# Four split slots instead of two for the weight parts of a two-block sequence model

## What is computed

```python
# first block, x [1, 512, 1024], mem [1, 256, 1024]
x = x + token_mixer(rmsnorm(x), w_in, ...)      # HGRN scan + mLSTM, two directions, @ w_out
x = x + cross_attention(rmsnorm(x), rmsnorm(mem), w_xq, w_xkv, w_xo)
x = x + square(relu(rmsnorm(x) @ w_up)) @ w_down
x = rmsnorm(x)
# second block
a = rmsnorm(x); proj = a @ w_in_2
y_att = windowed_gqa(rope(q), rope(k), v, sink) @ w_branch_attn
y_gla = gla_branch(...) @ w_branch_gla
h = x + (sigmoid(g_att) * y_att + sigmoid(g_gla) * y_gla) @ w_out_2
h = h + expert_choice_ffn(rmsnorm(h), ...)      # 16 experts, 64 tokens each
h = h + sigmoid(rmsnorm(h) @ w_ple_gate) * (p @ w_ple)
out = rmsnorm(h)
```

## Time and profile before

| what | value |
|---|---|
| median of 3 runs | 1978.03 us (1977.91 to 1978.99) |
| the profiled execution's own time | 1978.96 us |
| its span, first to last instruction | 1977.2 us |
| PE, POOL, DVE, ACT busy | 96%, 50%, 39%, 28% of the span |
| mean granted TensorE clock | 0.995 |

### The profile page before, as it was taken

One profiled execution on the slowest core, in us unless ns is written; L12 is line 12 of the kernel. 1 busy time (PEld: TensorE's weight loads), 2 busy tenths in 40 slices (PEclk: granted clock), 3 DMA queues, 4 the chain that ended last, 5 costly groups with the idle time before them and its releaser, 6 DMA issues.

```text
span 1977.2 us, 23272 instructions
## 1 busy us (share of the span) xinstructions
PE 1902.2 (96%) x9434; PEld 1394.3 (71%) x9434; DVE 778.3 (39%) x1187; ACT 554.4 (28%) x1122; POOL 994.2 (50%) x566
## 2 busy tenths in 40 slices
PE   7999998999999999999989999999999999999988
PEld 6888887688788888887867678887854444433436
DVE  2456668641423302433544365554241221221124
ACT  4535547331422101211133433342230000000025
POOL 5697867667278877887645496546600000000022
PEclk9999999999999999999999999999999999999999
DMA  5321124222133223222322222112699999999982
GB/s 183 96 75 43 44 75 139 85 73 98 33 96 96 96 96 96 96 96 86 119 64 64 65 77 84 54 64 75 270 362 421 421 421 422 420 421 421 421 348 74
DMA packets 92697, 335.81 MB, mean 170 GB/s; under 512 B 7696, under 2 KB 9488, under 8 KB 67760
## 3 DMA queue, kind: packets, MB, share of 16 engines
q1 hardware_dynamic: 88864, 321.29, 43.6%
q10 hardware_dynamic: 3584, 12.52, 1.7%
q0 software_dynamic: 144, 0.52, 0.1%
HBM read 328.01 MB, written 6.29 MB: 169 GB/s over the span
## 4 chain that ended last, share of the span: by engine, by line
PE 82%; DMA 7%; POOL 4%; DVE 3%; ACT 2%; issue 1%; SPq 1%; PEldq 0%; ACTq 0%; DVEq 0%; PEld 0%; POOLq 0%
PE bank L609 51%; PE bank L1867 12%; DMA arena<-in_w_exp_up 3%; PE bank L1898 3%; PE bank L786 2%; DMA shared<-in_w_exp_up 1%; DMA arena<-in_w_exp_gate 1%; DMA arena<-in_w_exp_down 1%; PE bank L630 1%; PE bank L1885 1%; POOL shared_r L667 1%; POOL shared_r L649 1%; PE bank L1071 1%; POOL shared_r L648 1%; PE bank L1453 1%
## 5 line engine op out<-in xcount | busy, mean ns | idle before, releaser
L609 PE MATMUL bank<-shared_r 128*128 128x512 f32 (+1 forms) x3888 | 899.0, 388 | 15.9 <-POOL shared_r L667 6.6
L609 PEld LDWEIGHTS bank<-shared_r 128*128 128x128 f32 x3888 | 704.8, 189 | 171.4 <-issue 16.7
L648 POOL TENSOR_TENSOR shared_r<-shared,small 128x1024 fp32r<-128x1024 f32 (+1 forms) x170 | 331.2, 1948 | 848.1 <-DMA shared<-in_w_ple_gate 493.7
L649 POOL TENSOR_TENSOR shared_r<-shared,shared_r 128x1024 fp32r<-128x1024 f32 (+1 forms) x170 | 419.3, 2466 | 13.4
L1867 PE MATMUL bank<-shared,arena 128*64 128x512 f32 x768 | 170.8, 595 | 9.5 <-DMA shared<-in_w_exp_gate 3.0
L1867 PE MATMUL bank<-arena 128*64 128x512 f32 x768 | 170.5, 595 | 9.8 <-DMA arena<-in_w_exp_up 4.0
L609 PE MATMUL bank<-shared_r,arena_r 128*128 128x512 f32 x768 | 176.1, 391 | 0.0
L609 PEld LDWEIGHTS bank<-shared_r,arena_r 128*128 128x128 f32 x768 | 144.2, 188 | 31.5
L667 POOL TENSOR_TENSOR shared_r<-shared,shared_r 128x1024 fp32r<-128x1024 f32 x42 | 106.9, 2547 | 76.8 <-ACT shared_r L658 76.7
L1867 PEld LDWEIGHTS bank<-shared,arena 128*64 128x64 f32 x768 | 57.4, 137 | 117.0 <-issue 106.6
L1867 PEld LDWEIGHTS bank<-arena 128*64 128x64 f32 x768 | 56.0, 137 | 117.3 <-issue 103.2
(11 more groups left out here) (429 smaller groups left out, 2086.1 us busy)
## 6 DMA issues: line engine op xcount, KB each, us to landing
shared<-in_w_in SPq DMA_DIRECT2D x80, 512.0 KB, 3.6
arena<-in_w_exp_gate SPq DMA_DIRECT2D x32, 1024.0 KB, 25.4
shared<-in_w_exp_gate SPq DMA_DIRECT2D x32, 1024.0 KB, 25.7
shared<-in_w_exp_up SPq DMA_DIRECT2D x32, 1024.0 KB, 23.4
arena<-in_w_exp_up SPq DMA_DIRECT2D x32, 1024.0 KB, 24.0
arena<-in_w_exp_down SPq DMA_DIRECT2D x32, 1024.0 KB, 25.5
shared<-in_w_exp_down SPq DMA_DIRECT2D x32, 1024.0 KB, 26.1
shared<-in_w_up SPq DMA_DIRECT2D x32, 512.0 KB, 3.6
```

Source lines behind the costliest of these rows:

```text
L609: ins = pe.matmul(dst, W_, x_, start=first, stop=final)
L648: link(pool.tensor_tensor(hi, raw(p), small[:, 18:19].to_broadcast([P, hi.shape[1]]), ALU.add))
L649: pool.tensor_tensor(lo, raw(p), hi.bitcast(F32), ALU.subtract).then_inc(S_("w_split"), 1)
```

## The change

Every weight part but those of the last stage gets one of four split slots instead of one of two. The two new ones lie in a new tile `spare` of 16 KB per partition. Its room comes from the descriptors' reserve, which is set to 1024 bytes per partition in place of the default, and from `arena`, shortened by 192 floats. `slot_free` waits for the part four before. The parts of `ple_gate` keep their slots and waits. The number of raw slots stays four, and no stream is reordered.

```diff
-ARENA = 26960
+ARENA = 26768
...
     X = sb("X", [P, ST, D])
+
+    spare_at = -(-nc.sbuf_base // 32) * 32
+    spare = sb("spare", [P, 2 * XPANEL])
+    spare_r = nc.alloc_sbuf_tensor_at("spare_r", [P, 2 * XPANEL], F32R, offset=spare_at)
...
             return arena_r[:, at:at + n], arena_r[:, at + n:at + 2 * n]
+        if p < late and parts[p]["split"] % 4 > 1:
+            at = 2048 * (parts[p]["split"] % 2)
+            return spare_r[:, at:at + n], spare_r[:, at + n:at + 2 * n]
         return shared_r[:, at:at + n], shared_r[:, at + n:at + 2 * n]
...
-        before = p - 6 if p >= late else split_parts[max(parts[p]["split"] - 3, 0)]
-        if parts[p]["split"] > 2 and (p < late or before >= late):
+        before = p - 6 if p >= late else split_parts[max(parts[p]["split"] - 5, 0)]
+        if parts[p]["split"] > 4 and (p < late or before >= late):
             part_done(eng, before)
...
-    nc = _bacc.Bacc("TRN2", target_bir_lowering=False, num_devices=1)
+    nc = _bacc.Bacc("TRN2", target_bir_lowering=False, num_devices=1, dynamic_dma_scratch_size=1024)
```

## The result

| kernel | median (range, runs) | ratio to before, 95% interval |
|---|---|---|
| before | 1978.65 us (1977.91 to 1980.93, 9) | |
| after | 1984.69 us (1983.22 to 1988.5, 9) | 1.0033 [1.0022, 1.0043] |

The profiled execution of the changed kernel took 1984.63 us (span 1982.9), 5.7 us more than that of the kernel before. Lines of the changed kernel are 7 higher than before: L616 is L609, L655 and L656 are L648 and L649, L674 is L667.

What follows compares the result with a forecast made beforehand. It took PE to bound the kernel, busy 1902.2 of 1977.2 us, with its waits for POOL's splits within reach. Gains 2.57 + 0 + 2.42 + 0.7 = 5.7 us took 1978.03 to 1972.3 us; range 1967.5 to 1978.0.

Steps and rivals of the forecast that it cites:

- the one behind `proj_a`: At DVE's rotation: it starts 1.0 us earlier, PE asks for it only afterwards, so the 2.42 us gain passes on.
- the four places: `proj_h`, `xk`, `proj_a` with `z`, and `gatt` with the start of `yatt`, where PE waits for POOL's splits.
- My own sign of being wrong: Matmuls from `spare_r` at 0.229 us or more, new PE waits in `hgrn` or attention, or a shifted DVE chain before `yatt`.
- `proj_h`, 2.57: In `proj_h`: both PE waits for POOL go, gaining 2.57 us, and `hgrn` behind it moves along; bounds 0 and 2.57.
- `xk`, 0: In `xk`: earlier splits meet the same DVE chain, gain 0; bounds a 2.5 us loss and a 3.6 us gain.
- the bound of one collision (2.5): In `xk`: the worst case, one more collision between POOL and DVE, costs 2.5 us.
- `proj_a` and `z`, 2.42: In `proj_a` and `z`: earlier splitting removes PE's waits of 0.85 and 1.25 us, gaining 2.42 us; bounds 1.01 and 2.42.
- `gatt` and `yatt`, 0.7: Before `yatt`: one 3.5 us wait replaces six small ones, gaining 2.35 us less 1.65 for half clock; other end 2.35.
- The reserve and the place of the halves, 0: Smaller descriptor reserve costs 0; reading half the parts from `spare` costs 0, bounds 0 and 5 to 17 us.
- The expert stage: Behind `ygla`: loads start when PE's `ygla` is evacuated, so its DMA and PE shift together.
- Splits move onto DVE's chain: Where DVE sets PE's pace, POOL's pair costs up to 4.3 us; slower from two places, 1980.9 us; chance 0.06.

Runs made afterwards that it cites:

- experiment 8: Changed kernel with the look-back of four parts only in `proj_h`, two elsewhere; 1975.99 us, 0.9988 of the kernel before.
- experiment 2: Changed kernel, but POOL splits two parts of `proj_g`, then waits until DVE has posted the rotation; 1977.22 us, 0.9991 of the kernel before.
- experiment 4: Changed kernel with the look-back of four parts only in `proj_a` and `proj_g`, two elsewhere; 1989.82 us, 1.0057 of the kernel before.
- experiment 6: Changed kernel with the look-back of four parts in `proj_h`, `down0` to `proj_a`, `gatt` and `yatt`, two elsewhere; 1971.34 us, 0.9956 of the kernel before.
- experiment 7: Changed kernel with the look-back of four parts only from `down0` to `proj_a`, two elsewhere; 1975.67 us, 0.9985 of the kernel before.
- experiment 9: Changed kernel with the look-back of four parts only from `down0` to `proj_g`, two elsewhere; 1985.42 us, 1.0036 of the kernel before.
- experiment 1: Changed kernel with its memory layout kept, but waiting for the part two before everywhere; 1978.54 us, 1.000 of the kernel before.
- experiment 3: Changed kernel with the look-back of four parts only in `proj_h`, `proj_a`, `gatt` and `yatt`, two elsewhere; 1976.17 us, 0.9984 of the kernel before.
- experiment 5: Changed kernel, look-back of four in `proj_h` and `down0` to `proj_r`, two elsewhere, POOL held in `proj_g` until the rotation is posted; 1972.45 us, 0.9962 of before.
- experiment 10: Changed kernel with the look-back of four parts only in `gatt` and `yatt`, two elsewhere; 1977.44 us, 0.9993 of the kernel before.

## Why the prediction was wrong, point by point

The step that failed is the one behind `proj_a`: "The rotation on DVE that follows ends at 990.4 ... and it starts from `proj_a`, so 1.0 us earlier ... the gain passes on". It started 0.6 us earlier (977.72 against 978.30) and ended 9.7 us later (1000.13 against 990.43). The size of the miss is this one step, 8.2 us. Under it lies a premise that I used three times: outside the four places "POOL splits one part, at the same moments as before", and "POOL's moments outside the four places don't change". That holds while POOL waits for PE at every part. Behind the `z` weights it didn't: POOL had a backlog, and each of its parts came as soon as a slot allowed. There the look-back alone made the pause of 2.35 us at 988 to 990, and that pause was in the trace that I read. My own sign of being wrong came true as well: `hgrn` and the rotation ahead of attention show new waits of PE (1.65 and 6.67 us).

Term by term:

- *`proj_h`, 2.57.* Right: both waits went. Measured 3.0 (experiment 8). But "`hgrn` begins with work ... so it moves along" is wrong for this kernel, where ACT and POOL enter `hgrn` with more slots: 2.2 us were lost at its end, 5.0 in the trace of experiment 2, which has the same code there.
- *`xk`, 0.* The trace shows -1.6 us, within the bound of one collision (2.5). At the transposes (L1034 / L1041) PE waited 2.73 us for ACT instead of 0.93. The waits behind them went, PE was through `xk` 4.1 us early (337.65 against 341.76 at the matmuls of L1052 / L1045), and then it waited 2.82 us for `xv`'s first part, whose two operations POOL made in 4.02 and 4.28 us beside DVE; behind that wait the granted clock is 0.50 for 5.5 us. Not all of it belongs to the change: experiments 4, 6, 7 and 9, which have two slots' look-back there, show a wait of 1.27 at the same place, the kernel before and experiments 1, 3, 5, 8 and 10 none. In these four the last part of `xk` ran at the full clock (24 matmuls in 3.14 us instead of 4.3 to 4.6) and PE reached `xv` up to 1.5 us earlier, too early for POOL. Why the clock stayed up there is open.
- *`proj_a` and `z`, 2.42.* Right: 2.5 in the traces.
- *`gatt` and `yatt`, 0.7.* The mechanism was right, a wait for the scans' last operation (L2627) in place of the small ones. Its size was off: 2.07 us and not 3.5, because a wait of 1.14 for ACT (L2384) that I hadn't seen came ahead of it. And behind it the clock stayed at 1.00, so that the 1.65 us that I had taken off didn't come. The step was 2.2 to 2.3 us in every trace with four slots there, at the other end of my bounds. That the clock stayed up isn't assured: in experiment 2 a wait of 2.04 us at this place was followed by a slower clock, and `yatt`'s first part took 7.42 us instead of 5.87.
- *The reserve and the place of the halves, 0.* Right: ratio 1.000 (experiment 1), and 389 ns at the median for `shared` with `spare`.
- *The expert stage, "its DMA and PE shift together".* Off by 1.3 us. `p` is loaded by ACT; SP's expert loads now begin 1.4 us behind its issue instead of 12.3, and it landed 19.4 us after its issue instead of 10.4. Experiment 2, with four slots there too, shows the same (1.4 and 20.1 us); experiments 3, 5 and 6, with two slots in `ygla` and `out2`, are as before (12.3 us, landing after 10.3 to 10.6) and have no such wait. That the loads ahead of it in time slow it down is argued from these pairs; no run moved them alone.

Of the rivals, "Splits move onto DVE's chain" is what happened, and I gave it 0.06. I priced it at one pair of POOL's operations, 4.3 us, and said that it needs two places. One place alone cost 8.2 us, more than all the gains together (7.6): DVE's chain of twelve two-input operations pays POOL's whole row of splits, as long as POOL doesn't pause. Had I counted the operations of the chain and the length of POOL's possible row (four slots and what PE frees meanwhile, six parts in the end, at 4.4 us each from 972.46 on), I would have seen that the row can reach past 993. My argument against the rival was the premise that failed.

The medians fit the parts. With the three gains alone (2.97, 3.29 and 1.14 from experiments 8, 7 and 10) the sum is 7.4 us, and experiment 6, which joins them, measured 7.6. The changed kernel has the same gains and in its own trace 8.2 + 2.2 + 1.6 + 1.3 = 13.3 us of losses, against 2.9 + 2.5 + 2.2 = 7.6 of gains: 5.7 in all, the difference of the two spans (steps of up to 0.4 us between the places cancel). The cause of the 8.2 is shown by experiments 2 and 9. For the 2.2 at `hgrn`'s end and the 1.3 at `p` the runs show that they go with two slots there (experiments 3, 6 and 8 for `hgrn`); how they come about is read from rows.

## What to carry to other kernels

A wait of an engine that is ahead isn't worthless: it may be the only pause in which another engine, whose operations collide with its own, gets its chain done. Before buffers are added, look for chains of short DVE operations that TensorE waits for, and ask whether GpSimd, set free, works through them without a gap; price that by the number of operations in the chain, not by one collision. Here more buffers paid only where they were given per stage: four slots where TensorE waited for splits, two elsewhere, with the growth placed where DVE isn't on the path, gave 0.9956 where four everywhere gave 1.0033.

## What the runs showed of the hardware that I had not expected

- An operation of DVE of 128x64 elements lasts 0.22 us with POOL silent and up to 2.38 us beside POOL's splits; one of 128x4 (L555, experiment 3) 0.17 against 1.82. In these rows the size of the DVE operation plays no part: it lasts until POOL's operation ends. L555 has a single tensor input, and so has L1271, whose 2.49 us I had put under the rule for two inputs; the Trainium skill (SBUF — State Buffer, "Who interferes with whom") names such `tensor_scalar` operations too, in their two-port mode, and the trace agrees with it in that L555 was held up. In which mode it ran no run shows.
- PE's wait of 2.04 to 2.08 us ahead of `yatt` was followed by a granted clock of 1.00 in five traces (the changed kernel and experiments 3, 5, 6 and 10), and in experiment 2, after 2.04 us, by 0.68 over the next 3.3 us. The shorter one of 1.78 to 1.81 in `xk` was followed by 0.50 in the kernel before, and by the full clock in experiments 4, 6, 7 and 9. So between 1.8 and 2.1 us the length of a wait doesn't tell whether the clock falls.
- Profiled executions with the same code in a stage differ by up to 3 us in `proj_h` (the first part in 7.33 or 5.68 us with the clock, and waits beside it). A term of 2 us is better read as a step at its place than from the ends of two traces.
